# The samples' vectors through DRAM on GpSimd's queue instead of the sync engine's, in a two-layer hybrid decoder step

## The chip, the cores and the metric

One Trainium2 chip, one core of it. The metric is the device time of one execution in microseconds (us). The program is one launch that holds both layers.

## The reference

Two layers, each run over a prompt group (256 tokens) and a sample group (8 sequences, one new token each), 264 columns in all, with D = 1024 and f32 throughout:

```python
def hybrid_layer(x, st, pos0, P, l):
    xn = rms_norm(x, P['ln1_g'][l])
    proj = (xn @ P['w_in'][l])
    y_a, ... = rwkv7_mixer(proj[..., :o1], ...)      # state S (value, key), 4 heads of 64
    y_b, ... = hgrn2_mixer(proj[..., o1:o2], ...)
    y_c, ... = retention_mixer(proj[..., o2:o3], ...)
    y_d, ... = mlstm_mixer(proj[..., o3:o4], ...)
    gates = sigmoid(proj[..., o4:]).reshape(B, T, 4, D)
    merged = sum(gates * (ys @ w_branch), axis=2)
    x = x + merged @ P['w_out'][l]
    x = x + peer_ffn(rms_norm(x, P['ln2_g'][l]), ...) # top-16 of 128x128 experts, 8 heads
```

For the eight samples each of the four mixers does one step of its recurrence on a 64x64 state per head: the state is decayed, a product of a key and a value is added, and it is read with a query. These steps are the place that the change touches.

## The kernel before

Everything is laid out with channels on partitions and the 264 columns along the free axis. The five engines run hand-ordered programs (one function each, from `@block.sync` to `@block.vector`) tied by semaphores; each loop over `l` is written out for both layers.

**Weights.** The sync engine (SP) asks for 1 MB blocks of two column tiles each (`block_of`, the DMA at L409) into four slots of `ring`. Before each it waits for the slot's `w_free`, which ScalarE raises once it has evicted the slot's second tile. A layer takes 44 blocks: 16 for the mixers' 32 column tiles, 16 for the 32 gate tiles (two tiles per block, numbered 0 to 31 here), then 4 each for the branch, the output and the query projections. SP's list is strict: what stands first in its program is issued first, and a wait holds up all behind it.

**The gate tiles as filler.** TensorE places gate tiles (`gate_products`, matmuls at L581, each listed as two records, so 16 records a tile) in the gaps of the mixers' chains. Their number at each place is fixed: 14 of them before the samples' step, then `GATES_AT = (4, 5, 2, 1)` at four places within it, then six. ScalarE evicts them at L1040 in its own fixed order.

**The samples' step (layer by layer).**

1. VectorE has gathered 18 vectors per sample and head pair in `sv`. ScalarE adds the last two (L1135, L1136), TensorE transposes them (L799, L800), and ScalarE copies them out as `svt` and `svt2` (L1138, L1139), raising `act_step` to `act_svt`.
2. SP waits for that, writes both to `scratch` in DRAM (L426, 96 rows of 1 KB; L427, 48 rows of 1 KB), waits for both to land (`sp_svw`), reads them back as `gv` (L429: 128 partitions, each 18 pieces of 64 bytes) and as `gvv` (L432, four DMAs of 128 partitions with 256 bytes each), and only then goes on: the `shift` output (L435), and the next weight block, number 24, with gate tiles 16 and 17.
3. VectorE waits for all five reads (`sp_svr`) and runs the step: L1583 and L1584 give `sa`; L1585 to L1590 decay the states and add the new products; L1592 needs TensorE's sum over quads (L805, which needs `sa`); L1594 to L1608 end with `po`.
4. TensorE turns `po` back (L809, L810), VectorE normalises up to L1621 (`dve_yy`), and TensorE goes on with the means (L816), the variances (L824), the last gate tiles and the branch, output and query projections (L838, L852, L869).

TensorE's order through it:

```python
e.transpose(...svt...)                # L799, L800
gate_tiles(GATES_AT[0])               # tiles 14 to 17
e.wait_ge(S("dve_sa"), 1); mm(...)    # L805
gate_tiles(GATES_AT[1])               # tiles 18 to 22
e.wait_ge(S("dve_po"), 1); mm(...)    # L809, L810
gate_tiles(GATES_AT[2])               # tiles 23, 24
```

GpSimd multiplies and adds for the second mixer early in a layer (L1246, L1252) and has nothing to do after that until VectorE's routing (L1751) lets it copy indices (L1256) and fetch expert rows with indirect DMAs (L1266).

Of the kernel before, what the change touches and what calls it, by code (L numbers as in the profile page):

```python
# [22 lines left out]
NS = 8  # L23
# [3 lines left out]
HD = 64  # L27
# [51 lines left out]
V_F, V_K, V_Q, V_V, V_RW = 0, 3, 6, 9, 12  # L79
RW_W, RW_K, RW_R, RW_KK, RW_KKA, RW_V = range(12, 18)  # L80
NVEC = 18
NGLA = 12
# [72 lines left out]
def build(nc, A, O):  # L155

    with ExitStack() as ctx:
# [5 lines left out]
        def sem(name, per_layer=True):  # L163
            s = ctx.enter_context(nc.semaphore(name))
            if per_layer:
                sems[name] = s
            return s
# [38 lines left out]
        def carve(*shape, at=None, dt=F32):  # L206
            n = int(np.prod(shape))
            if at is None:
                at = top[0]
                top[0] += n  # L210
            assert at + n <= ARENA, (at, n)
            v = arena[:, at:at + n]
            if dt != F32:
                v = v.bitcast(dt)
            if len(shape) == 1:
                return v
            names = " ".join(f"d{i}" for i in range(len(shape)))
            return v.rearrange(f"p ({names}) -> p {names}", **{f"d{i}": s for i, s in enumerate(shape)})
# [54 lines left out]
        svt, svt2 = carve(PR, P), carve(PR, P)  # L273
        gv = carve(NVEC, 16)
        gvv = carve(4, HD)
# [52 lines left out]
        def row(k):  # L328
            return ring[:, k, :] if k < 4 else low_rows[:, k - 4, :]
# [3 lines left out]
        for name in (  # L333
                "act_co act_cv act_ps act_q act_silu act_step act_top act_var act_wa act_wag act_y "
                "dve_att dve_cm dve_cum dve_cv dve_dt dve_hg dve_inv dve_kk2 dve_kr dve_kw dve_mg dve_pm "
                "dve_hb dve_hk dve_hp dve_ht dve_hs dve_hy dve_po dve_qk dve_qz dve_r dve_r1 dve_rk dve_route dve_rows dve_sa dve_sbd dve_shift dve_st dve_sv "
                "dve_top dve_u dve_x dve_xs dve_y dve_yc dve_yn dve_yy "
                "pe_cf pe_cm pe_co pe_ctr pe_hh pe_ks pe_p pe_ps pe_s pe_sc pe_y pe_step pe_t pe_u pe_var pe_wo "
                "pe_wq dve_hid pe_acc pe_xa act_acc "
                "pool_hg pool_hy "  # L340
                "sp_dfin sp_hfin sp_keys sp_ln sp_out sp_par sp_rw sp_sr sp_svr sp_svw sp_sw ").split():
            sem(name)
        once = {name: sem(name, False) for name in ("sp_once", "act_const", "dve_lb", "act_lb", "dve_sq", "pe_ss", "act_rt", "dve_xn")}

        def S(name):
            return once[name] if name in once else sems[name]
# [11 lines left out]
        def step(name):  # L358

            steps = PE_STEPS if name.startswith("pe_") else ACT_STEPS  # L360
            return steps.index(name.split("_")[1]) + 1

        def take(e, s, n):

            e.wait_ge(s, n)
            e.sem_clear(s)
# [26 lines left out]
        def bc(ap, k, shape):  # L393
            return ap.unsqueeze(k).to_broadcast(shape)

        @block.sync
        def _(e):
            e.dma_start(const[:, 0:FIRST], A["const"][:, 0:FIRST]).then_inc(S("sp_once"), 16)
            e.dma_start(x[:, :, :], A["x"]).then_inc(S("sp_once"), 16)
            for l in range(L):  # L400
# [5 lines left out]
                def block_of(j, n):  # L406

                    take(e, w_free[j], 1)
                    e.dma_start(ring[:, j, :], A["w"][bass.ds(n, 1)].rearrange("a p c -> p (a c)")).then_inc(w_full[j], 16)  # L409
# [11 lines left out]
                e.dma_start(O["p_rw"][bass.ds(l, 1)].rearrange("a p c -> p (a c)"), state2[:, NCH % 2, :, :].rearrange("p a b -> p (a b)")).then_inc(S("sp_rw"), 16)  # L421
                for j in range(4):
                    block_of(j, l * N_BLOCKS + N_MIXED + 4 + j)

                e.wait_ge(S("act_step"), step("act_svt"))
                e.dma_start(O["scratch"][0:NGLA * NS, :], svt[0:NGLA * NS, :, :].rearrange("p a b -> p (a b)")).then_inc(S("sp_svw"), 16)  # L426
                e.dma_start(O["scratch"][NGLA * NS:NVEC * NS, :], svt2[0:(NVEC - NGLA) * NS, :, :].rearrange("p a b -> p (a b)")).then_inc(S("sp_svw"), 16)  # L427
                e.wait_ge(S("sp_svw"), 32)
                e.dma_start(gv[:, :, :], O["scratch"].rearrange("(v b) (q k) -> (b q) v k", v=NVEC, k=16)).then_inc(S("sp_svr"), 16)  # L429
                for n, v in enumerate((V_V, V_V + 1, V_V + 2, RW_V)):  # L430
                    src = O["scratch"][v * NS:(v + 1) * NS, :].rearrange("b (h c) -> (b h) c", c=HD)
                    e.dma_start(gvv[:, n, :], bc(src, 1, [32, 4, HD])).then_inc(S("sp_svr"), 16)  # L432

                e.wait_ge(S("dve_shift"), 1)
                e.dma_start(O["shift"][bass.ds(l, 1)].rearrange("a p c -> p (a c)"), out_shift[:, :, :].rearrange("p a b -> p (a b)")).then_inc(S("sp_out"), 16)  # L435
# [795 lines left out]
        @block.gpsimd  # L1231
        def _(e):
            own = Own(e, "pool_own")
            tt_ = e.tensor_tensor
            for k in range(SLOT):
                e.sem_inc(row_free[k], 1)
            for l in range(L):
                own.clear()

                e.wait_ge(S("dve_hg"), 1)  # L1240
                sub = lambda t: proj[:, t:t + 2, 0:SEQ].rearrange("p a (c w) -> p a c w", w=SUB)
                for j in range(1, SUB):
                    before = sub(HG) if j == 1 else pairs[j - 1]
                    if j > 1:
                        e.wait_ge(S("pool_hg"), j - 1)
                    tt_(pairs[j], before[:, :, :, 1:], sub(HG + 2)[:, :, :, 1:SUB + 1 - j], ALU.mult).then_inc(S("pool_hg"), 1)  # L1246
                y_sub = yy[:, 2:4, 0:SEQ].rearrange("p a (c w) -> p a c w", w=SUB)
                for j in range(1, SUB):
                    e.wait_ge(S("dve_ht"), j + 1)
                    if j > 1:  # L1250
                        e.wait_ge(S("pool_hy"), j - 1)
                    tt_(y_sub[:, :, :, j:], y_sub[:, :, :, j:], pairs[j], ALU.add).then_inc(S("pool_hy"), 1)  # L1252
                own.clear()

                def indices(par, src):
                    own(e.tensor_copy(ix[:, par, :], src))  # L1256

                def fetch(par, first=False):

                    for k in range(SLOT):  # L1260
                        if first and k < 4:
                            e.wait_ge(S("pe_wq"), 2 * k + 2)
                        if first and k == 4:
                            e.wait_ge(S("pe_ps"), PH + 2)
                        take(e, row_free[k], 1)
                        e.indirect_dma_start(out=row(k), out_offset=None, in_=A["uv"],  # L1266
                                             in_offset=bass.IndirectOffsetOnAxis(ap=ix[:, par, k:k + 1], axis=0)).then_inc(row_full[k], 16)

                for tt in range(TT):
                    for g in range(GROUPS):  # L1270
                        e.wait_ge(S("dve_route"), ROUTED[tt][g])
                        with e.Fori(0, PER_GROUP // 2 - (tt == 1 and g == GROUPS - 1)) as i:
                            own.clear()
                            for par in range(2):
                                indices(par, eidx[:, tt, bass.ds(i * 16 + g * GH * TOPK + SLOT * par, SLOT)].bitcast(U32))
                                fetch(par, tt == g == par == 0)
                        own.clear()
                for par, n in ((0, SAMPLES_AT - 1), (1, None), (0, SAMPLES_AT)):
                    if n is None:
                        e.wait_ge(S("sp_sr"), 32)  # L1280
                        indices(par, es)
                    else:
                        indices(par, eidx[:, 1, n * SLOT:n * SLOT + SLOT].bitcast(U32))
                    fetch(par)
                e.sem_inc(arrive, 1)
                take(e, go["pool"], 1)

        @block.vector
        def _(e):
# [3 lines left out]
            def bank(b, n=N, lo=0, p0=0, p1=P):  # L1293
                return ps[p0:p1, b, lo:lo + n]
# [33 lines left out]
            for l in range(L):  # L1328
# [70 lines left out]
                r, k, v = raw[:, 0:2, :], raw[:, 2:4, :], raw[:, 4:6, :]  # L1399
# [66 lines left out]
                for c in range(NCH):  # L1466
                    tt, q = divmod(c, 2)
# [65 lines left out]
                for j in range(4):  # L1533
                    for t in range(4):
                        w = V("cw", 4 * t + j)
                        src = cpad[:, t, j:j + 288]
# [26 lines left out]
                for h in range(H):  # L1563
                    src = bank(h // 2, SEQ, SEQ * (h % 2))
# [9 lines left out]
                causal(1, lambda tt: small[:, 16 + 4 * tt:20 + 4 * tt])  # L1574
                e.sem_inc(S("dve_sv"), 1)

                e.wait_ge(S("sp_svr"), 16 * 5)
                rw, gla = st[:, 3, :, :], st[:, 0:3, :, :]

                def over_v(v, n=1):  # L1580
# [360 lines left out]
```

## Time and profile before

| | us |
|---|---|
| median of 3 runs | 2303.49 (2302.83 to 2306.79) |
| the profiled execution, device time | 2315.07 |
| its span in the trace | 2313.3 |
| TensorE, matmul busy | 1739.4 (75%) |
| VectorE busy | 1323.5 (57%) |
| ScalarE busy | 710.1 (31%) |
| GpSimd busy | 721.2 (31%) |
| mean granted clock of TensorE | 0.802 |

A trace is one execution; its times are from the span's start. "Idle before" is the time that an engine stood still before an instruction, with what ended it. "Remote" there, and "another core or an unknown queue" in the chain, stand for a release that the trace puts down to no instruction. The chain of work that ended last is followed back from the last instruction. Windows list busy time per engine and TensorE's granted clock as a share of 2.4 GHz.

### The profile page before, as it was taken

The page shows a single profiled execution, that of the slowest core. Times are in us where ns is not written, and L with a number is a line of the kernel's source. Part 1 is how long each engine was busy: PE and PEld are TensorE (multiplying, and loading weights), DVE is VectorE, ACT ScalarE, POOL GpSimd, SP SyncE. Part 2 cuts the span into 40 slices and gives each one's busy share as a digit, 9 for nine tenths or more (in the row PEclk, how much of TensorE's full clock was granted, in tenths as well). Part 3 has the DMA queues.
Part 4 walks back from the last instruction along what each step waited for, and adds up shares of the span by engine and source line. Part 5 has one row for each costly group of instructions (what it writes and reads, how often), then busy time and mean ns, then how long its engine had stood idle before and what let it go on. Part 6 is the DMA issues. An engine that isn't in the chain of part 4 may idle for free.

```text
span 2313.3 us, 28575 instructions
## 1 busy us (share of the span) xinstructions
PE 1739.4 (75%) x9812; PEld 901.8 (39%) x9812; DVE 1323.5 (57%) x3085; ACT 710.1 (31%) x2080; POOL 721.2 (31%) x658
## 2 busy tenths in 40 slices
PE   7999889975665666666699888899666667666666
PEld 6777678741111111111178776787211111111112
DVE  2335464456767676685433353655567775766854
ACT  2211222043333333333321203310433333333433
POOL 0400000035454554545322000000544545455452
PEclk9999899987667776767799998999876766676765
DMA  6320143479999999999753210443999999999996
GB/s 260 127 92 4 75 144 132 155 291 421 421 421 421 419 421 420 420 406 407 322 209 128 75 58 24 171 144 112 370 421 421 422 421 421 421 421 420 401 420 252
DMA packets 102187, 665.72 MB, mean 288 GB/s; under 512 B 20000, under 2 KB 21952, under 8 KB 22208
## 3 DMA queue, kind: packets, MB, share of 16 engines
q0 software_dynamic: 76032, 553.68, 57.9%
q1 hardware_dynamic: 24352, 107.35, 12.8%
q10 hardware_dynamic: 1696, 3.40, 0.4%
q8 instruction: 51, 0.84, 0.1%
q14 instruction: 56, 0.46, 0.1%
HBM read 657.80 MB, written 6.58 MB: 287 GB/s over the span
## 4 chain that ended last, share of the span: by engine, by line
PE 38%; DMA 35%; DVE 13%; issue 6%; ACT 4%; POOL 3%; another core or an unknown queue 0%; SPq 0%; POOLq 0%; ACTq 0%; DVEq 0%
DMA arena<-in_uv,arena 21%; DMA ring<-in_uv,arena 14%; PE ps L518 9%; PE ps L581 7%; PE ps L906 6%; PE ps L869 3%; PE ps L838 2%; PE ps L852 2%; DVE arena L1772 2%; DVE ring L1772 2%; POOL arena L1266 2%; POOL ring L1266 1%; ACT arena L1197 1%; ACT arena L1196 1%; PE ps L527 1%
## 5 line engine op out<-in xcount | busy, mean ns | idle before, releaser
L906 PE MATMUL ps<-arena 64*64 64x512 f32 x2112 | 428.3, 906 | 255.9 <-ACT arena L1197 255.0
L906 PE MATMUL ps<-ring,arena 64*64 64x512 f32 x2112 | 405.6, 884 | 220.1 <-ACT arena L1197 208.7
L1772 DVE SCALAR_TENSOR_TENSOR arena<-arena 128x1024 f32<-128x1024 f32 x264 | 322.2, 1226 | 223.1 <-DMA arena<-in_uv,arena 212.5
L1772 DVE SCALAR_TENSOR_TENSOR ring<-ring,arena 128x1024 f32<-128x1024 f32 x264 | 319.3, 1225 | 216.4 <-DMA ring<-in_uv,arena 181.6
L1266 POOL DMA_INDIRECT arena<-in_uv,arena x264 | 332.3, 1259 | 352.3 <-PE ps L906 287.3
L1266 POOL DMA_INDIRECT ring<-in_uv,arena x264 | 313.5, 1187 | 294.2 <-PE ps L906 222.1
L1195 ACT ACTIVATE arena<-arena 128x1 f32<-128x1 f32 x528 | 107.0, 203 | 782.8 <-DVE arena L1772 405.0
L906 PEld LDWEIGHTS ps<-arena 64*64 64x64 f32 x2112 | 74.2, 173 | 580.9 <-issue 580.9
L906 PEld LDWEIGHTS ps<-ring,arena 64*64 64x64 f32 x2112 | 83.5, 178 | 551.7 <-issue 551.0
L1256 POOL COPY arena<-arena 128x8 uint32 (+1 forms) x66 | 25.1, 381 | 747.3 <-DVEq L1751 746.9
L581 PE MATMUL ps<-xn,ring 128*128 128x264 f32 x1024 | 244.4, 397 | 14.4 <-remote 12.3
L518 PE MATMUL ps<-xn,ring 128*128 128x264 f32 x1024 | 239.6, 395 | 8.5 <-ACTq L988 5.1
L581 PEld LDWEIGHTS ps<-xn,ring 128*128 128x128 f32 x1024 | 197.0, 195 | 51.9 <-issue 17.2
L518 PEld LDWEIGHTS ps<-xn,ring 128*128 128x128 f32 x1024 | 198.3, 195 | 47.9 <-DVE xn L1310 9.1
L1197 ACT ACTIVATE arena<-const,arena 128x64 f32<-128x64 f32 x528 | 184.0, 349 | 17.7
L1196 ACT ACTIVATE arena<-arena 128x1 f32<-128x1 f32 x528 | 155.4, 294 | 17.5
L993 ACT ACTIVATE arena<-ps 128x264 f32<-128x264 f32 x64 | 25.3, 395 | 226.4 <-PE ps L518 226.3
L1040 ACT ACTIVATE arena<-ps 128x264 f32<-128x264 f32 x50 | 19.3, 390 | 204.7 <-PE ps L581 204.3
L869 PE MATMUL ps<-xn,ring 128*128 128x264 f32 x256 | 64.4, 410 | 5.9 <-DVE xn L1310 5.9
L1246 POOL TENSOR_TENSOR arena<-arena 128x480 f32<-128x480 f32 (+14 forms) x30 | 28.3, 942 | 126.6 <-DVEq L1345 124.4
L838 PE MATMUL ps<-arena,ring 128*128 128x264 f32 x256 | 57.5, 387 | 2.0 <-remote 2.0
L869 PEld LDWEIGHTS ps<-xn,ring 128*128 128x128 f32 x256 | 51.9, 204 | 16.2 <-DVE xn L1310 6.7
(398 smaller groups left out, 1687.1 us busy)
## 6 DMA issues: line engine op xcount, KB each, us to landing
ring<-in_w SPq DMA_DIRECT2D x88, 1024.0 KB, 4.8
ring<-in_uv,arena POOLq DMA_INDIRECT x264
arena<-in_uv,arena POOLq DMA_INDIRECT x264
st<-in_st SPq DMA_DIRECT2D x2, 2048.0 KB
out_st<-st SPq DMA_DIRECT2D x2, 2048.0 KB
const<-in_const ACTq DMA_DIRECT2D x1, 2667.0 KB, 11.8
arena<-in_keys SPq DMA_DIRECT2D x2, 1024.0 KB, 6.9
x<-in_x SPq DMA_DIRECT2D x1, 1056.0 KB, 4.9
```

Source lines behind the costliest of these rows:

```text
L518: m = mm(bank(b), ring[:, j, at:at + P], xn[:, kt, :], start=kt == 0, stop=kt == KT - 1)
L581: m = mm(bank(b), ring[:, j, at:at + P], xn[:, kt, :], start=kt == 0, stop=kt == KT - 1)
L838: m = mm(bank(b), ring[:, j, at:at + P], yy[:, 2 * m_ + k, :], start=k == 0, stop=k == 1)
L852: m = mm(bank(6 + o % 2), ring[:, j, at:at + P], src[:, kt, :], start=kt == 0, stop=kt == KT - 1)
L869: m = mm(bank(6 + o % 2), ring[:, o // 2, at:at + P], xn[:, kt, :], start=kt == 0, stop=kt == KT - 1)
L906: m = mm(ps[chunk(q ^ half), 2 * tt + half, :], dg[chunk(q), k, :], row(k)[chunk(q), D + 512 * half:D + 512 * half + 512], start=False, st ...
L1195: own(act(hge[:, k:k + 1], hid[:, k:k + 1], ACT.Gelu))
L1196: own(act(hgg[:, k:k + 1], hge[:, k:k + 1], ACT.Copy, scale=gate))
L1197: act(dg[:, k, :], C("channel"), ACT.Copy, scale=hgg[:, k:k + 1]).then_inc(dg_full[k], 1)
L1246: tt_(pairs[j], before[:, :, :, 1:], sub(HG + 2)[:, :, :, 1:SUB + 1 - j], ALU.mult).then_inc(S("pool_hg"), 1)
L1266: e.indirect_dma_start(out=row(k), out_offset=None, in_=A["uv"], in_offset=bass.IndirectOffsetOnAxis(ap=ix[:, par, k:k + 1], axis=0)).then ...
L1772: stt(u, u, 1.0, xtok[:, tt, :], ALU.mult, ALU.mult, accum_out=hid[:, k:k + 1]).then_inc(S("dve_hid"), 1)
```

## The change

The scratch DMAs leave SP's program, with SP's wait for `act_svt` and for the writes, and stand in GpSimd's behind its adds (L1252). Their semaphores are new, not cleared between the layers, and so waited for with values that grow with `l`. VectorE waits for the new one.

```diff
@@ @block.sync
                 for j in range(4):
                     block_of(j, l * N_BLOCKS + N_MIXED + 4 + j)
-
-                e.wait_ge(S("act_step"), step("act_svt"))
-                e.dma_start(O["scratch"][0:NGLA * NS, :], svt[0:NGLA * NS, :, :].rearrange("p a b -> p (a b)")).then_inc(S("sp_svw"), 16)
-                e.dma_start(O["scratch"][NGLA * NS:NVEC * NS, :], svt2[0:(NVEC - NGLA) * NS, :, :].rearrange("p a b -> p (a b)")).then_inc(S("sp_svw"), 16)
-                e.wait_ge(S("sp_svw"), 32)
-                e.dma_start(gv[:, :, :], O["scratch"].rearrange("(v b) (q k) -> (b q) v k", v=NVEC, k=16)).then_inc(S("sp_svr"), 16)
-                for n, v in enumerate((V_V, V_V + 1, V_V + 2, RW_V)):
-                    src = O["scratch"][v * NS:(v + 1) * NS, :].rearrange("b (h c) -> (b h) c", c=HD)
-                    e.dma_start(gvv[:, n, :], bc(src, 1, [32, 4, HD])).then_inc(S("sp_svr"), 16)
 
                 e.wait_ge(S("dve_shift"), 1)
@@ @block.gpsimd
                     tt_(y_sub[:, :, :, j:], y_sub[:, :, :, j:], pairs[j], ALU.add).then_inc(S("pool_hy"), 1)
+                e.wait_ge(S("act_step"), step("act_svt"))
+                e.dma_start(O["scratch"][0:NGLA * NS, :], svt[0:NGLA * NS, :, :].rearrange("p a b -> p (a b)")).then_inc(S("pool_svw"), 16)
+                e.dma_start(O["scratch"][NGLA * NS:NVEC * NS, :], svt2[0:(NVEC - NGLA) * NS, :, :].rearrange("p a b -> p (a b)")).then_inc(S("pool_svw"), 16)
+                e.wait_ge(S("pool_svw"), 32 * (l + 1))
+                e.dma_start(gv[:, :, :], O["scratch"].rearrange("(v b) (q k) -> (b q) v k", v=NVEC, k=16)).then_inc(S("pool_svr"), 16)
+                for n, v in enumerate((V_V, V_V + 1, V_V + 2, RW_V)):
+                    src = O["scratch"][v * NS:(v + 1) * NS, :].rearrange("b (h c) -> (b h) c", c=HD)
+                    e.dma_start(gvv[:, n, :], bc(src, 1, [32, 4, HD])).then_inc(S("pool_svr"), 16)
                 own.clear()
@@ @block.vector
-                e.wait_ge(S("sp_svr"), 16 * 5)
+                e.wait_ge(S("pool_svr"), 16 * 5 * (l + 1))
```

## Rows read from the trace of the kernel before

**Rows 1.** The chain that ended last, layer 0: start us, us, what
```profile
303.75 6.74 another core or an unknown queue
310.57 10.22 PE ps L581 x32
...
339.30 1.08 PE ps L809 x8
```

**Rows 2.** The chain that ended last, layer 1
```profile
1444.73 0.33 SPq L426
...
1449.87 2.16 DMA arena<-scratch
1452.05 1.24 DVE arena L1583
...
1484.64 1.08 PE ps L809 x8
```

**Rows 3.** The chain that ended last, layer 0, behind L810
```profile
340.60 7.20 PE ps L581 x32
347.80 1.78 PE ps L816 x8
```

**Rows 4.** Timeline of layer 0: start us, us, engine, line, operation [idle before]
```profile
295.27 0.39 ACT L1040 ACTIVATE arena<-ps 128x264 f32<-128x264 f32 x1 [3.31 <-PE ps L581]
...
297.33 0.33 SPq L426 DMA_DIRECT2D scratch<-arena  x1
297.71 1.77 SPq L427 DMA_DIRECT2D scratch<-arena  x1
...
305.00 0.65 ACT L1040 ACTIVATE arena<-ps 128x264 f32<-128x264 f32 x2
305.36 30.61 SPq L409 DMA_DIRECT2D ring<-in_w  x7
305.79 1.23 DVE L1583 TENSOR_TENSOR arena<-st,arena 128x1024 f32<-128x1024 f32 x1 [20.13 <-DMA arena<-scratch]
307.05 1.87 DVE L1584 TENSOR_REDUCE arena<-arena 128x64 f32<-128x1024 f32 x1
...
320.80 18.02 PE L581 MATMUL ps<-xn,ring 128*128 128x264 f32 x80
...
321.08 0.23 DVE L1592 TENSOR_SCALAR arena<-ps 128x64 f32<-128x64 f32 x1 [0.96 <-PE ps L805]
...
346.41 0.71 DVE L1621 TENSOR_TENSOR arena<-arena 128x528 f32<-128x528 f32 x1
```

**Rows 5.** Timeline of layer 1
```profile
1445.11 0.42 SPq L427 DMA_DIRECT2D scratch<-arena  x1
...
1446.78 0.39 SPq L429 DMA_DIRECT2D arena<-scratch  x1
...
1447.21 3.27 SPq L432 DMA_DIRECT2D arena<-scratch  x4
...
1456.60 8.95 PE L581 MATMUL ps<-xn,ring 128*128 128x264 f32 x32 [5.45 <-remote]
```

**Rows 6.** GpSimd's timeline, layer 0
```profile
99.28 0.73 POOL L1252 TENSOR_TENSOR arena<-arena 128x64 f32<-128x64 f32 x2 [2.92 <-DVE arena L1358]
473.53 0.19 POOL L1256 COPY arena<-arena 128x8 uint32 x1 [373.52 <-DVEq L1751]
...
478.87 0.94 POOL L1266 DMA_INDIRECT ring<-in_uv,arena  x1 [0.30 <-issue]
```

**Rows 7.** GpSimd's queue: packets, MB, share of 16 engines
```profile
q0 software_dynamic: 76032, 553.68, 57.9%
```

**Rows 8.** DMA issues: engine, operation, count, KB each, median us to landing
```profile
arena<-scratch SPq DMA_DIRECT2D x8, 32.0 KB, 2.2
...
arena<-scratch_g SPq DMA_DIRECT2D x2, 4.0 KB, 8.8
```

**Rows 9.** Windows: PE, PEld, DVE, ACT, POOL busy, then PE clock, DMA share, GB/s
```profile
310.57:320.79 10.22, 10.21 (x34) 8.31 (x35) 9.51 (x5) 0.39 (x1) 0.00 (x0) 0.72 0.67 273
...
1456.60:1465.55 8.95, 8.95 (x34) 7.42 (x35) 8.92 (x5) 0.39 (x1) 0.00 (x0) 0.82 0.74 309
```

More of the change, by code:

```diff
@@ L340, in build @@
                 "pool_hg pool_hy "
-                "sp_dfin sp_hfin sp_keys sp_ln sp_out sp_par sp_rw sp_sr sp_svr sp_svw sp_sw ").split():
+                "sp_dfin sp_hfin sp_keys sp_ln sp_out sp_par sp_rw sp_sr sp_sw ").split():
             sem(name)
-        once = {name: sem(name, False) for name in ("sp_once", "act_const", "dve_lb", "act_lb", "dve_sq", "pe_ss", "act_rt", "dve_xn")}
+        once = {name: sem(name, False) for name in ("sp_once", "act_const", "dve_lb", "act_lb", "dve_sq", "pe_ss", "act_rt", "dve_xn", "pool_svw", "pool_svr")}
         def S(name):
```

## The prediction

> **What bounds the kernel now.** I read the chain of waits first. In layer 0 it goes through TensorE: the chain holds 6.74 us of a release by no instruction, then 32 records of L581 in 10.22 us, and ends this section at L809, 339.30 us [rows 1]. The timeline says what that release is: SP asks for the next weight blocks only at 305.36 [rows 4], behind the whole scratch trip, so tiles 16 and 17 start at 310.57, when block 24 has landed. Taken alone this promises 6.74 us. In layer 1 the chain goes another way, through SP's write (1444.73), the last read, VectorE from 1452.05, and L809 at 1484.64 [rows 2], although TensorE waits 5.45 us for a block there too [rows 5]. So TensorE and VectorE arrive nearly together. Layer 0 shows how nearly: VectorE waits for TensorE's L805 just 0.96 us [rows 4], and TensorE ends its five tiles at 320.80 + 18.02 = 338.82, 0.48 before L809 starts.
>
> VectorE's side is a plain sum in both layers: scratch landed, then 33.51 us to L809 in layer 0 (305.79 to 339.30) and 32.59 in layer 1 (1452.05 to 1484.64); the 0.96 is the difference. The trip through DRAM therefore stands on the path whole. It takes 305.79 - 297.33 = 8.46 us in layer 0 and 1452.05 - 1444.73 = 7.32 in layer 1. Behind L810 only TensorE bounds: L581 for 7.20 us, then L816 [rows 3], while VectorE has its input for L816 ready at 346.41 + 0.71 = 347.12, 0.7 us before L581 is over.
>
> **What goes.** SP no longer waits for `act_svt`. Slot 0 is free once tile 9 is evicted, long before, so blocks 24 and 25 come early, and block 26 at about 295.7, behind tile 13's eviction at 295.27 [rows 4]. TensorE's wait for block 24 goes. Next late is the eviction of tile 14: ScalarE has other work until 305.00 [rows 4]. TensorE then runs tiles 16 and 17 at its full rate, 7.20 us [rows 3], to about 312.5, and L805 is no longer late. The gain on the path is 0.96 us in layer 0 and nothing in layer 1. The rest turns into waiting for VectorE further on, before L809.
>
> The `shift` write and SP's other work also move ahead; nothing waits for them. Two semaphores fewer to clear, and waits with larger constants, I cost at nothing: the clearing stands behind GpSimd's and TensorE's last work of the layer, and if it were not covered it would be tenths of a us.
>
> **What stands behind GpSimd's new waits.** GpSimd is idle from about 100.0 to 473.53 [rows 6], and layer 1 repeats it, so its wait for `act_svt` and for its own writes holds up nothing. The copy of indices and the fetches that stand behind it come 160 us later.
>
> **What the trip costs on GpSimd's queue.** No plain DMA is issued from GpSimd in this trace. The nearest row is its indirect fetch, 0.94 us of issue each with 0.30 between two [rows 6]; the queue's count, 76032 packets for 528 fetches, is 144 each, about one per row of 128 [rows 7]. I take 0.94 for a DMA of about 128 pieces and no pause, since the pause there also holds a semaphore's take. SP's own issues take 0.33 to 0.82 [rows 2, 5].
>
> - Writes: 2 x 0.94 = 1.88, then landing. In layer 1 the reads are issued 1446.78 - 1445.53 = 1.25 us after the second write's issue ended [rows 5]. Together 3.13.
> - `gv`: 128 x 18 = 2304 pieces in one instruction. If the issue is a fixed cost it is 0.94; if it goes by pieces, 18 x 0.94 = 16.9. SP issues it in 0.39 [rows 5], but GpSimd's queue is of another kind, software_dynamic [rows 7]. Neither end is nearer; I take the geometric middle, 4.0.
> - `gvv`: 4 x 0.94 = 3.76.
> - Last landing: 1452.05 - (1447.21 + 3.27) = 1.57.
>
> Sum 3.13 + 4.0 + 3.76 + 1.57 = 12.46 us. Block 26 is now in flight when the writes go out, and block 27 (free with tile 15's eviction) when the last reads do. A scratch read lands in 2.2 us on quiet queues and in 8.8 amid the fetches [rows 8]; one block in flight is much less than those. I add 0.5 per direction, bounds 0 and 3 for the trip. So 13.5 us, which is 5.0 more than layer 0's 8.46 and 6.2 more than layer 1's 7.32: 11.2 in all.
>
> **A rule against the row.** The row gives 0.94 for 128 rows and leaves open how it grows. The Trainium skill, DMA: Bandwidth & Descriptors, section on the anatomy of one DMA on the gpsimd path, says that generating descriptors is small and that many can be emitted before the added cost shows. By it `gv` would be near 0.94, and the sum below +8.9 instead of +15.0; no run here shows which. The same page gives about 1 us to the first byte from gpsimd against 0.6 from sync, which speaks against the change by an estimated 0.8 us a layer (two trips in a row) even where issue is cheap.
>
> **The clock.** Once TensorE has stood still 6.8 us (layer 0) or 5.45 us (layer 1), it comes back at a granted clock that averages 0.72 and 0.82 over the next two tiles [rows 9], a mix of 2.4 and 1.2 GHz; they take 10.22 and 8.95 us instead of 7.20 [rows 1, 5, 3]: 3.0 and 1.75 more. Before, this fell ahead of L805, where layer 0 paid the 0.96 counted above and layer 1 nothing. Now the stand moves ahead of L809. With `sa` ready at 308.92 + 5.0 = 313.9, five tiles of 3.6 us end at 332, and L809 can start at 339.30 - 0.96 + 5.0 = 343.3: 11 us idle, in layer 1 much the same. The slow tiles then stand behind L810, where TensorE is the bound. I add the mean, 2.4 us, in each layer: 4.8 (bounds 3.5 and 6.0).
>
> **Sum:** 11.2 - 0.96 + 4.8 = +15.0 us. Against the profiled execution that is a span of 2313.3 + 15.0 = 2328.3 and a device time of 2330.1. That execution stands 11.6 above the median of the runs shown; against the median, 2303.49, I forecast 2318.5.
>
> **Rivals.**
>
> - *Issue is a fixed cost.* `gv` at 0.94 takes 3.06 off each layer: +8.9, 2312.4. For it: SP's issue does not grow with the pieces. Against it: the fetch, on the other kind of queue, costs 0.94 where SP's cheapest costs 0.33. Chance 0.28.
> - *Issue goes by pieces throughout.* `gv` at 16.9 adds 12.9 in each layer: +40.8, 2344.3 (with pauses of 0.30 and 3 us of crowding, up to +50). For it: the only row of this queue prices 128 rows at 0.94, well above SP's usual issue. Chance 0.20, counting from +23.
> - *GpSimd issues plain DMAs as SP does*, the trip is 7.32 in both layers: -1.14 - 0.96 + 4.8 = +2.7, 2306.2. Chance 0.12. The clock is then all that is left.
> - *Faster.* The trip itself shrinks, because GpSimd issues at SP's cheapest, 0.33 each, with nothing in front: 2 x 0.33 + 1.25 + 5 x 0.33 + 1.57 = 5.13, so -3.3 and -2.2, with the 0.96 -6.5, and the clock holds: 2297.0. It decides where the two trips and the clock together cost less than -3.6. The chain's 6.74 speaks for it at first sight; that VectorE is only 0.96 behind, and that no GpSimd row is under 0.9, against. Chance 0.03.
> - *That the blocks do not come early* I give nothing: nothing else stands ahead of them in SP's list but the `shift` write, whose input is ready.
>
> **The numbers.** The forecast's case (`gv` between 2 and 8 us, total +11 to +23) has 0.37. A change of less than 0.2% (4.6 us) is about what a measurement can't tell from none. Same: 0.10, most of the fourth case; faster 0.03; slower 0.87. The range goes from 2306, into the case of SP-like issue, to 2342, just short of the issue by pieces throughout; some 0.07 lies below and 0.12 above.
>
> **What would show it.** In the trace of the changed kernel: plain DMAs on GpSimd's queue behind L1252, with their durations, `gv` longest; L1583 starting 12 to 15 us after ScalarE's L1139; no wait of TensorE for block 24, but an idle of about 10 us before L809, and L581 behind L810 at some 9.6 us instead of 7.20. Right in size only if `gv` takes 2 to 8 us. Wrong if L1583 starts no later than before, if the trip is longer than 20 us, or if the two tiles behind L810 take 7.20 after such an idle.

## The result, and the profile after

The changed kernel takes 2316.59 us (median of 6 runs, 2312.28 to 2324.26) against 2303.8 for the kernel before in the same batches: a ratio of 1.0064, 95% interval 1.0044 to 1.0084, so 10 to 19 us slower. The profiled execution has a device time of 2323.71 and a span of 2321.9; the one of before had 2313.3.

The chain that ended last, layer 0 (start us, us, what), answers to [rows 1, 3]:

```profile
298.72 0.74 POOL scratch L1245
299.45 4.61 DMA scratch<-arena
...
304.35 1.27 POOL arena L1248
...
307.22 5.94 DMA arena<-scratch
...
313.18 1.24 DVE arena L1582
...
345.62 1.91 PE ps L800 x8
347.53 0.43 PE ps L801 x2
347.96 8.64 PE ps L572 x32
356.59 1.78 PE ps L807 x8
```

Layer 1, which answers to [rows 2]:

```profile
1452.90 1.27 POOL arena L1248
...
1455.76 5.09 DMA arena<-scratch
...
1460.87 1.24 DVE arena L1582
...
1493.33 1.92 PE ps L800 x8
1495.25 0.43 PE ps L801 x2
1495.67 9.91 PE ps L572 x32
```

Line numbers have moved: L1245 and L1246 are the writes, L1248 reads `gv`, L1251 `gvv`, L1582 is VectorE's first step, L796 the sum over quads, L572 the gate tiles, L800 and L801 the products with `po`, L807 the means. The detour over TensorE in layer 0 is gone; both layers now run GpSimd, DMA, VectorE, TensorE. What has grown is two pieces named DMA: 4.61 us behind the writes and 5 to 6 us behind the reads, where the chain of before, in layer 1, had 1.66 and 2.16. And the two tiles behind L801 take 8.64 and 9.91 us, 7.20 before.

The timeline of layer 0 shows who else was at work (answers to [rows 4]):

```profile
296.33 37.21 SPq L409 DMA_DIRECT2D ring<-in_w  x5
...
299.45 0.55 POOL L1246 DMA_DIRECT2D scratch<-arena  x1
...
304.35 1.27 POOL L1248 DMA_DIRECT2D arena<-scratch  x1 [4.35 <-DMA scratch<-arena]
...
305.62 2.20 POOL L1251 DMA_DIRECT2D arena<-scratch  x4
...
306.62 7.38 PE L572 MATMUL ps<-xn,ring 128*128 128x264 f32 x32 [1.78 <-ACT arena L1031]
...
313.18 1.22 DVE L1582 TENSOR_TENSOR arena<-st,arena 128x1024 f32<-128x1024 f32 x1 [26.74 <-DMA arena<-scratch]
...
345.62 1.91 PE L800 MATMUL ps<-const,arena 128*128 128x32 f32 x8 [9.27 <-DVE arena L1607]
```

SP asks for block 26 at 296.33, 2.4 us ahead of the first write. TensorE no longer waits for block 24 but 1.78 us for ScalarE's eviction, as forecast, and then stands still 9.27 us ahead of L800. The issues themselves are cheap: 0.75 and 0.55 us for the writes, 1.27 for `gv`, 2.20 for all four `gvv`. VectorE stood still during all of them (26.74 us idle ahead of L1582), so no run here shows what an issue from GpSimd costs beside VectorE's work. Block 27 is asked for at 305.27, just ahead of the first `gvv`.

TensorE's granted clock from the products with `po` to the means, layer 0 and layer 1 (columns as in [rows 9]):

```profile
345.62:356.43 10.81, 10.81 (x43) 9.35 (x43) 6.33 (x10) 0.39 (x1) 0.00 (x0) 0.76 0.17 55
1493.33:1505.42 12.09, 12.09 (x43) 10.21 (x43) 6.33 (x10) 0.39 (x1) 0.00 (x0) 0.68 0.16 53
```

In the kernel before both stretches take 8.34 us at 1.00.

For the two layers, with the section taken from the first write's issue to the means' first matmul:

| us, layer 0 / layer 1 | before | after | difference |
|---|---|---|---|
| trip: first write's issue to VectorE's start | 8.46 / 7.32 | 14.46 / 12.71 | +6.0 / +5.4 |
| VectorE's start to the products with `po` | 33.51 / 32.59 | 32.44 / 32.46 | -1.07 / -0.13 |
| products with `po` to the means | 8.34 / 8.34 | 10.81 / 12.09 | +2.47 / +3.75 |
| section | 50.31 / 48.25 | 57.71 / 57.26 | +7.4 / +9.0 |

The section loses 16.4 us. The spans differ by 8.6 only, because the rest of the span came out shorter (2206.9 against 2214.7). That rest differs as much without the change: over the profiled executions of all kernels below that have the same tile order it lies between 2200.0 and 2216.7. The medians, 12.8 apart (10 to 19 by the interval), agree with the section.

### The profile page after: what moved, and what is told of

Same layout as the page of the kernel before. It is cut to its first block, busy times and chain, and to the rows that moved or that the text cites. A ratio compares the mean times of both kernels' runs of the same rounds, so it can differ in the third digit from the quotient of the medians.

```text
span 2321.9 us, 28571 instructions
## 1 busy us (share of the span) xinstructions
PE 1738.8 (75%) x9812; PEld 905.6 (39%) x9812; DVE 1323.4 (57%) x3085; ACT 710.2 (31%) x2080; POOL 732.0 (32%) x672
## 3 DMA queue, kind: packets, MB, share of 16 engines
q1 hardware_dynamic: 18208, 106.49, 12.8%
## 4 chain that ended last, share of the span: by engine, by line
PE 37%; DMA 37%; DVE 14%; issue 5%; ACT 4%; POOL 2%; another core or an unknown queue 0%; POOLq 0%; DVEq 0%; ACTq 0%; SPq 0%
DMA arena<-in_uv,arena 18%; DMA ring<-in_uv,arena 17%; PE ps L509 9%; PE ps L572 6%; PE ps L897 5%; PE ps L860 3%; PE ps L829 2%; PE ps L843 2%; DVE ring L1771 2%; DVE arena L1771 2%; POOL ring L1265 1%; ACT arena L1188 1%; ACT arena L1187 1%; POOL arena L1265 1%; PE ps L518 1%
## 5 line engine op out<-in xcount | busy, mean ns | idle before, releaser
L572 PE MATMUL ps<-xn,ring 128*128 128x264 f32 x1024 | 246.7, 400 | 5.6 <-ACT arena L1031 3.5
L509 PEld LDWEIGHTS ps<-xn,ring 128*128 128x128 f32 x1024 | 198.5, 195 | 47.3 <-DVE xn L1309 8.6
L572 PEld LDWEIGHTS ps<-xn,ring 128*128 128x128 f32 x1024 | 198.7, 197 | 43.5 <-issue 8.4
L1245 POOL DMA_DIRECT2D scratch<-arena x2 | 1.4, 682 | 395.8 <-ACT arena L1130 395.8
```

What stands on the lines that cost most here:

```text
L509: m = mm(bank(b), ring[:, j, at:at + P], xn[:, kt, :], start=kt == 0, stop=kt == KT - 1)
L572: m = mm(bank(b), ring[:, j, at:at + P], xn[:, kt, :], start=kt == 0, stop=kt == KT - 1)
```

## The experiments

All ratios are to the kernel before on the same chip, with 95% intervals. Each trip and section is from one profiled execution. In every kernel that holds weight blocks back or sends them ahead, the loop over blocks 24 to 31 is also written out; the diffs printed here leave most of that out.

### Is it the queue, or the traffic beside it?

*pool_none_early*: the changed kernel, but SP waits for the reads first.

```diff
@@ @block.sync, behind blocks 20 to 23
+                e.wait_ge(S("pool_svr"), 16 * 5 * (l + 1))
                 e.wait_ge(S("dve_shift"), 1)
```

> The scratch DMAs stay on GpSimd's queue as in the changed kernel, but the sync engine waits for the five reads before it asks for block 24, so no weight block is in flight during the trip through DRAM. Theory A, crowding: the changed kernel's trip (14.46 and 12.71 us from the first write's issue to VectorE's start, against 8.46 and 7.32 before) is long because blocks 26 and 27 share the DMA engines with it; here it falls to about 8 us in both layers, TensorE waits for block 24 again, and the time is that of before within 3 us, about 2304. Theory B, the queue: the trip is as long on GpSimd's queue by itself; it stays at 12 to 14 us and the time is about 2315.

Measured: 2303.74 us against 2300.97, ratio 1.0012 (0.9998 to 1.0026). Its timeline in layer 0:

```profile
298.83 0.55 POOL L1250 DMA_DIRECT2D scratch<-arena  x1
...
301.20 1.27 POOL L1252 DMA_DIRECT2D arena<-scratch  x1 [1.82 <-DMA scratch<-arena]
...
302.47 2.19 POOL L1255 DMA_DIRECT2D arena<-scratch  x4
...
306.47 1.23 DVE L1586 TENSOR_TENSOR arena<-st,arena 128x1024 f32<-128x1024 f32 x1 [20.29 <-DMA arena<-scratch]
306.92 2.06 SPq L409 DMA_DIRECT2D ring<-in_w  x4
```

The same instructions with the same durations, and the wait for the writes is 1.82 us, not 4.35; VectorE starts 1.81 us after the last read's issue has ended, not 5.36. Trips: 8.37 and 8.04 us. So GpSimd's queue costs -0.1 and +0.7 us against SP's, and the blocks in flight 6.1 and 4.7. Theory A holds: crowding, as I call it from here on.

The lists of DMA issues say that it goes both ways. In layer 0 of the changed kernel (305 to 314 us; KB each, median us from issue to landing):

```profile
ring<-in_w SPq DMA_DIRECT2D x1, 1024.0 KB, 7.0
arena<-scratch POOLq DMA_DIRECT2D x4, 32.0 KB, 6.0
```

and in that of pool_none_early (302 to 307 us):

```profile
arena<-scratch POOLq DMA_DIRECT2D x4, 32.0 KB, 2.7
```

The first of these is block 27; the median block lands in 4.8 us. The 16 DMA engines are 91% to 96% busy from 306 to 310 us in the changed kernel, 32% to 33% from 302 to 306.5 in pool_none_early. No run separates the engines from the memory behind them.

*pool_two_early*: blocks 24 and 25 ahead of that wait.

```diff
+                block_of(0, l * N_BLOCKS + N_MIXED + 8)
+                block_of(1, l * N_BLOCKS + N_MIXED + 9)
+                e.wait_ge(S("pool_svr"), 16 * 5 * (l + 1))
                 e.wait_ge(S("dve_shift"), 1)
...
+                block_of(2, l * N_BLOCKS + N_MIXED + 10)
+                block_of(3, l * N_BLOCKS + N_MIXED + 11)
+                for j in range(4):
+                    block_of(j, l * N_BLOCKS + N_MIXED + 12 + j)
```

> As the changed kernel, but only blocks 24 and 25, whose slots are free long before, are asked for ahead of the trip; block 26 waits for the five reads. Crowding (A): trip about 8 us, no wait of TensorE for block 24, an idle of about 7 us before the products with po, a fallen clock behind them at 2 to 4 us a layer: about 2308. Queue (B): trip 12 to 14 us, about 2316, the changed kernel's time.

Measured: 2311.78 against 2300.97, ratio 1.0045 (1.003 to 1.006). The trips are 8.24 and 8.15 us, short again with block 26 held back: crowding. TensorE waits for no block, stands 7.4 us ahead of the products with `po`, and takes 10.73 and 10.75 us from them to the means. The section sums to 4.3 us over before; the medians say 10.8, the interval 7 to 14, midway between the two expectations. The 3 us or more between section and time I did not find, so here the trips decide, not the time.

*pool_three_early*: the same with `block_of(2, ...)` ahead of the wait as well, so block 26 is in flight and block 27 is not.

> As pool_two_early, with block 26 asked for ahead of the trip, but block 27 held until the five reads have landed. Crowding by single blocks: block 26 delays the write only (from the second write's issue end to the first read's issue 4 us instead of 1.7), and the reads land as on quiet queues (from the last read's issue end to VectorE's start 1.6 to 2 us; in the changed kernel, with block 27 in flight, 5.4). Trip 10 to 11 us, time about half way between pool_two_early and the changed kernel. Rival, one block in flight delays both ways, or the reads are slow for another reason: reads land in 4 to 5 us here too.

Measured: 2309.06 against 2302.63, ratio 1.0034 (1.0018 to 1.0049). Layer 0:

```profile
295.35 0.33 SPq L409 DMA_DIRECT2D ring<-in_w  x1
...
298.32 0.55 POOL L1250 DMA_DIRECT2D scratch<-arena  x1
...
303.31 1.27 POOL L1252 DMA_DIRECT2D arena<-scratch  x1 [4.44 <-DMA scratch<-arena]
304.58 2.20 POOL L1255 DMA_DIRECT2D arena<-scratch  x4
...
308.57 1.23 DVE L1586 TENSOR_TENSOR arena<-st,arena 128x1024 f32<-128x1024 f32 x1 [22.94 <-DMA arena<-scratch]
```

The write waits 4.44 us as in the changed kernel; the reads land 1.79 us after their issue, as on quiet queues. So each way has its block: 26 costs the write (trips 10.99 and 9.08, against 8.24 and 8.15), 27 costs the reads (14.46 and 12.71, against 10.99 and 9.08). The time does not follow: half way between pool_two_early and the changed kernel was expected, as the sections ask (9.7 us over before against 4.3 and 16.4), and its ratio is the lowest of the three. The runs don't rank it against pool_two_early.

*sp_two_early* and *sp_three_early* do the same on SP's queue: the scratch DMAs stay where they were before, and two or three blocks go ahead of them (the diff is that of two).

```diff
@@ @block.sync, the kernel before
+                block_of(0, l * N_BLOCKS + N_MIXED + 8)
+                block_of(1, l * N_BLOCKS + N_MIXED + 9)
                 e.wait_ge(S("act_step"), step("act_svt"))
                 e.dma_start(O["scratch"][0:NGLA * NS, :], ...
```

> The kernel before with blocks 24 and 25 asked for ahead of the sync engine's wait, the scratch DMAs still on its own queue and no block in flight. Both theories: trip 7.3 to 8.5 us, VectorE no longer waits 0.96 us for the sum over quads. What it tells is the clock: if the idle that moves ahead of the products with po brings a fallen clock onto the path, the time is 2 to 5 us above that of before, about 2307 to 2308; if the clock costs nothing there, it is 1 us below before.

> As sp_two_early with block 26 asked for ahead of the wait too, so it is in flight (from about 296 us on) when the sync engine writes the scratch. Crowding (A): the write's landing grows from 1.3 to about 4 us and the trip by about 3 in each layer, time about 6 us above sp_two_early, 2314. Queue (B): the trip grows by less than 1 us, time within 2 us of sp_two_early.

Measured: 2307.71 against 2300.97, ratio 1.0031 (1.0017 to 1.0045), with trips of 8.84 and 7.45; and 2317.12, ratio 1.0068 (1.0048 to 1.0087), with trips of 11.13 and 9.32. Crowding is no matter of GpSimd's queue: with block 26 ahead, SP's own write waits too. Its timeline in layer 0:

```profile
296.16 0.33 SPq L409 DMA_DIRECT2D ring<-in_w  x1
...
298.53 0.55 SPq L430 DMA_DIRECT2D scratch<-arena  x1
...
303.87 0.39 SPq L432 DMA_DIRECT2D arena<-scratch  x1
```

That is 4.79 us from the second write's issue end to the first read's issue, and 3.38 in layer 1; in sp_two_early, on the same queue without a block in flight, it is 2.84 and 1.27. The two intervals of the time don't overlap.

And sp_two_early prices the clock nearly alone. No block is in flight, the trip is about that of before, and it is still 6.7 us slower (4 to 10 by the interval; 2 to 5 was expected). TensorE's timeline, layer 0 and layer 1:

```profile
339.73 1.91 PE L812 MATMUL ps<-const,arena 128*128 128x32 f32 x8 [7.75 <-DVE arena L1611]
341.88 10.16 PE L584 MATMUL ps<-xn,ring 128*128 128x264 f32 x32
...
1478.54 1.92 PE L812 MATMUL ps<-const,arena 128*128 128x32 f32 x8 [6.37 <-DVE arena L1611]
1480.69 9.09 PE L584 MATMUL ps<-xn,ring 128*128 128x264 f32 x32
```

The section says 6.0: 0.5 from the trips, -1.1 from the sum over quads that comes earlier, +6.6 between the products with `po` and the means (12.15 and 11.08 against 8.34, at granted clocks of 0.68 and 0.74).

### Is it the clock?

*after_filled* and *after_filled24*: the changed kernel with 18 or 24 matmuls more, which compute nothing that is used, where TensorE stands still (the diff is that of 18).

```diff
@@ @block.tensor, behind gate_tiles(GATES_AT[1])
+                for kt in range(18):
+                    mm(bank(6), C("ident"), xn[:, kt % KT, :], start=True, stop=True)
                 e.wait_ge(S("dve_po"), 1)
```

> The changed kernel with 18 matmuls more (128x264, f32, into a bank that nothing reads, 8.0 us at full rate), placed behind the five tiles, ahead of the products with po: TensorE works through its idle of 9.3 and 11.0 us. Nothing on the path changes but the clock. Theory of the clock: L816's place is 2.5 and 3.8 us closer to VectorE's last copy (the two tiles back to 7.2 us, the products with po to 1.1), and the time falls by about 6 us against the changed kernel, to 7 above before. Rival, that the slow rate has another cause (the wait itself, the weights' arrival): no change, 13 above before.

Measured: 2322.78 against 2301.88, ratio 1.0084 (1.0066 to 1.0101): a miss, 15 to 23 us above before where 7 was expected, though its section sums to 15.4 over before, 1 less than the changed kernel's. The trace says why the test was not clean. TensorE's timeline in layer 0:

```profile
345.16 1.08 PE L802 MATMUL ps<-const,arena 128*128 128x32 f32 x8 [1.45 <-DVE arena L1609]
346.07 0.39 PE L803 MATMUL ps<-const,arena 128*128 128x32 f32 x2
346.30 9.05 PE L572 MATMUL ps<-xn,ring 128*128 128x264 f32 x32
```

1.45 us were left idle here and 3.02 in layer 1, and the clock fell nevertheless, in layer 0 only among the gate tiles (the windows of 1 us grant 1.00 up to 347, 0.63 in the next, then 0.50). From the products with `po` to the means: 10.03 and 11.42 us, not 8.34. So the filler was made to reach all the way.

> after_filled left TensorE idle for 1.5 us (layer 0) and 3.0 us (layer 1) ahead of the products with po, and the granted clock fell all the same. Here the filler is 24 matmuls (10.7 us), up to the moment when po is ready. Theory of the clock: it stays at the full rate in both layers, 8.34 us from the products with po to the means as in the kernel before (10.81 and 12.09 in the changed one); layer 0's products come about 1.2 us late; 4 to 5 us below after_again. Rival, the slow rate behind po is not a matter of the idle: 10 to 12 us in that stretch, time at or above after_again.

> The changed kernel itself, unedited, beside the others of this batch, so that they can be held against it on the same chip. 11 to 16 us above before.

Measured: after_filled24 2315.45, ratio 1.0057 (1.004 to 1.0075); after_again, the changed kernel itself on that chip, 2317.36, ratio 1.0059 (1.0046 to 1.0072). TensorE's timeline of after_filled24, layer 0 and layer 1:

```profile
334.00 10.84 PE L799 MATMUL ps<-xn,const 128*128 128x264 f32 x48
344.68 0.97 PE L802 MATMUL ps<-const,arena 128*128 128x32 f32 x8
345.49 0.39 PE L803 MATMUL ps<-const,arena 128*128 128x32 f32 x2
345.71 7.37 PE L572 MATMUL ps<-xn,ring 128*128 128x264 f32 x32
...
1486.51 1.08 PE L802 MATMUL ps<-const,arena 128*128 128x32 f32 x8 [0.48 <-DVE arena L1609]
1487.43 0.39 PE L803 MATMUL ps<-const,arena 128*128 128x32 f32 x2
1487.65 7.37 PE L572 MATMUL ps<-xn,ring 128*128 128x264 f32 x32
```

With an idle of at most 0.48 us the stretch is back at 8.23 and 8.34 us and a granted clock of 1.00, against 11.09 and 12.04 us in after_again: the slow tiles are the clock's, and the clock's fall is the idle's. In the section that is worth 4.5 us net (57.69 and 56.84 down to 56.04 and 53.98, with 1.2 us paid for the filler in layer 0). The medians differ by 1.9 us where 4 to 5 were expected, less than they can resolve. The trace shows the mechanism; these two kernels don't size it in time. That rests on sp_two_early.

### Can the idle be used?

Three kernels with `GATES_AT = (4, 7, 2, 1)`: two gate tiles are moved from the end of the list into the place ahead of the products with `po`.

```diff
-GATES_AT = (4, 5, 2, 1)
+GATES_AT = (4, 7, 2, 1)
```

*before_tiles7*, the control:

> The control: the kernel before with the same seven tiles. TensorE has no idle to put them in (0.5 and 1.1 us ahead of the products with po), because it waits for block 24 instead. So the products with po come 6 to 7 us later, and the tiles only change places: within 2 us of before. If this alone gains over 5 us, the early blocks are not what gives the room.

Measured: 2297.76 against 2301.88, ratio 0.9982 (0.997 to 0.9995). The products with `po` come 6 us later (39.45 and 38.58 us after VectorE's start, not 33.51 and 32.59). A gain of 1 to 7 us where within 2 us was expected; an estimate from the section is 2.2 (12.0 us lost in it, 14.2 won by two tiles of 3.55 fewer in each layer behind it).

*after_tiles7*, the changed kernel:

> The changed kernel with the same seven tiles. The trip stays crowded (12.7 to 14.5 us), the idle shrinks to 2 to 4 us, so the clock should hold or nearly. 16.4 us lost in the section, 14.2 won back by the tiles and up to 6 by the clock: 0 to 5 us below before.

Measured: 2302.92 against 2301.88, ratio 0.9998 (0.9987 to 1.001), where 0 to 5 us below before was expected. The tiles win back what the trip loses. The clock held in layer 0 (8.34 us, after an idle of 2.25) and not in layer 1 (10.01, after 3.94).

*sp_two_tiles7*, sp_two_early with them, and *pool_two_tiles7*, pool_two_early with them:

> sp_two_early with seven gate tiles instead of five in the place ahead of the products with po, and four instead of six at the end. If that idle (6.4 to 7.8 us) is real slack of TensorE, the two tiles (7.1 us) fit in it, the clock holds, and TensorE, the bound from there on, has 7.1 us less to do in each layer: 14 to 15 us below before (about 2287), as the four tiles left still cover the 11 us of the variances' chain. Rival, VectorE or ScalarE is the bound behind the variances: less than 6 us gained.

> sp_two_tiles7 with the scratch on GpSimd's queue (blocks 24 and 25 early, block 26 held until the reads have landed, seven tiles ahead of the products with po). If the queue matters by 0.3 us a trip at most, the time is that of sp_two_tiles7 within 3 us, 13 to 16 us below before; if GpSimd's queue has a cost that the trips on quiet queues do not show, it is 5 us or more above it.

Measured: sp_two_tiles7 2286.53 against 2301.88, ratio 0.9941 (0.9918 to 0.9963); pool_two_tiles7 2290.6 against 2302.63, ratio 0.9948 (0.9935 to 0.9961). Both beat both kernels, and the queue makes no difference that these runs show. pool_two_tiles7 against after_tiles7 also prices the crowding in time, at one tile order: some 11 us between the two ratios (each to the kernel before on its own chip), whose intervals don't overlap, and 11.3 us between the sections (98.4 for both layers against 109.6), 1.7 of them the clock's. TensorE in layer 0 of sp_two_tiles7:

```profile
308.87 25.14 PE L584 MATMUL ps<-xn,ring 128*128 128x264 f32 x112
334.45 1.08 PE L812 MATMUL ps<-const,arena 128*128 128x32 f32 x8 [0.44 <-DVE arena L1611]
335.36 0.39 PE L813 MATMUL ps<-const,arena 128*128 128x32 f32 x2
335.58 7.37 PE L584 MATMUL ps<-xn,ring 128*128 128x264 f32 x32
```

Seven tiles at the full rate (25.14 us), an idle of 0.44, the two tiles behind it at 7.37: here the early blocks at last become time, because TensorE, the bound from there on, has two tiles less to do. Against before_tiles7, which has the tiles but not the early blocks, it is 11 us faster; the other 4 of its 15 us are the tiles' own.

## Why the prediction was right, point by point

- **Sign and range: right. Size: right, in part by luck.** +15.0 was forecast, 12.8 measured, 16.4 in the section's own sum; 2318.5 against 2316.59. The prediction made it a condition of being right in size that `gv` takes 2 to 8 us; it took 1.27, so the size came out for another reason than the one given.
- **What bounds:** right. The 6.74 us of the chain that a first look promises were worth 1.07 us in layer 0 (0.13 in layer 1): VectorE is next, as [rows 4] showed. The next wait behind it, ScalarE's eviction of tile 14, is in the trace (1.78 us).
- **The issue of the DMAs: mis-sized.** I took 9.64 us (two writes and four `gvv` at 0.94, `gv` at 4.0). It measured 0.75 + 0.55 + 1.27 + 2.20 = 4.77. The indirect fetch's 0.94 was the wrong row to scale from; a plain DMA of a like number of pieces takes 0.55 to 0.75. `gv`'s 2304 pieces cost 1.27, some 2.3 times a `gvv` with its 128, so of the ends 0.94 and 16.9 the lower was nearly the true one. The Trainium skill, DMA: Bandwidth & Descriptors, the section on the anatomy of one DMA on the gpsimd path, has many descriptors emitted before the cost shows; the trace agrees with that at 1.27 us. The Trainium skill's first-byte figures on the same page, 0.8 us a layer against the change as an estimate, are near too: pool_none_early gives -0.1 and +0.7.
- **Crowding: mis-sized the other way.** I took 0.5 us for each direction, 1.0 per trip, bounds 0 and 3. It is 6.1 and 4.7. The two rows at hand, a landing of 2.2 on quiet queues and 8.8 amid the fetches [rows 8], were read rightly as ends; to call one block in flight "much less" than the fetches was the step that failed. With a block in flight the reads took 6.0 us to land, not 2.2 or 2.7. That the two errors cancel is luck: in layer 0, 4.9 us too much for the issues against 5.1 too little for crowding and 0.8 too little for the landings on quiet queues. So 13.5 us were forecast for the trip, and 14.46 and 12.71 measured.
- **The clock:** right in place and nearly in size. 4.8 us forecast, 2.47 + 3.75 = 6.2 measured, after idles of 9.3 and 11.0 us (11 forecast). Layer 0's idle is shorter because TensorE also stands still 2.35 us ahead of the sum over quads there; the clock falls behind that too (0.58 from 316 to 320 us), and the five tiles take 19.70 us, not 18.02. That fall costs nothing, as TensorE still waits for VectorE behind them.
- **The rivals:** issue by pieces is out (`gv` would take 16.9). Of the two with cheap issues, the fixed cost is near for `gv` (0.94 against 1.27) and too dear for the other six (0.94 against 0.55 to 0.75). "GpSimd issues as SP does" is nearly what happens: 4.77 us of issue in all, where SP's in layer 1 took 4.41. Both sums miss the time because crowding is missing in the one and 1.0 a trip in the other. pool_two_early is the last case without crowding: its section is 4.3 us over before (10.8 by the medians), 2.7 in the rival's sum.

## What to carry to other kernels

When a transfer that others wait for moves to a queue of its own, what it left behind starts earlier, and 1 MB blocks are then in flight beside it. Hold back the blocks that fall into its flight, and let only those go early that land before it. A wait taken from an engine that was not alone at the bound moves that engine's idle further on; if the next work there is on the path, the clock's fall is paid in full. Early data pays only once there is work to put into the room that it makes: the same two early blocks cost 7 us with the old tile order (sp_two_early against before) and gained 11 with two tiles moved (sp_two_tiles7 against before_tiles7).

## What the runs showed of the hardware

Pieces and packets differ by queue. The page's section on DMA queues, after:

```profile
q0 software_dynamic: 76576, 554.53, 57.8%
q1 hardware_dynamic: 18208, 106.49, 12.8%
```

SP's queue (q1) lost 24352 - 18208 = 6144 packets, exactly 3072 a layer: 2304 + 4 x 128 + 96 + 48 pieces and 7 x 16. GpSimd's queue [rows 7] gained only 544 for the same transfers. The 144 packets per indirect fetch, from which the prediction read one per row, say nothing of plain DMAs.

The clock can fall after a short idle. It fell behind 1.45 us of idle in after_filled and behind 2.35 us ahead of the sum over quads in the changed kernel, and did not behind 2.25 us ahead of the products with `po` in after_tiles7 (8.34 us to the means, at 1.00). The idle's length, its place in time and the work around it changed together, so what decides there stays open.
